# Two transformer blocks on one core: several attentions run as one chain of duos that begins under the value projections

## The reference

```python
# first block
h = rms_norm(x, norm_mix)
aq, ak, av, bq, bk, bv, cq, ckv, cg, mg = split(h @ w_in)
oa = diff_attention(norm(aq), norm(ak), av, lam, bias_a)       # 4 heads, two maps each, causal; then rms_norm
ob = banded_attention(norm(bq), norm(bk), bv, bias_b, 128, sinks)   # 8 heads, window 128
oc = nsa_attention(norm(cq), kc, vc, ks, vs, kw, vw, gates, bias_c) # 8 heads: compressed + selected + window
x = x + sum_n(sigmoid(mg_n) * (o_n @ w_branch_n)) @ w_out
x = x + relu(rms_norm(x) @ w_up)**2 @ w_down
# second block, twice
x = x + 0.5 * mod * swiglu(modulate(rms_norm(x)))
h = modulate(rms_norm(x))
qa, ka, va, ub, qc, kc, vc, f, g = split(h @ w_in)
ya = chunked_relpos_attention(norm(qa), norm(ka), va)          # 8 heads
yb = multiscale_pool(ub)
yc = forgetting_attention(norm(qc), norm(kc), vc, f)           # 8 heads
x = x + mod * (sum_n(sigmoid(g_n) * (y_n @ w_branch_n)) @ w_out)
x = x + 0.5 * mod * swiglu(modulate(rms_norm(x)))
```

## Time and profile before

| | |
|---|---|
| median of 3 runs | 3509.34 us (3509.17 to 3512.36) |
| the profiled execution | 3509.4 us |
| its span, first to last instruction | 3507.6 us |
| mean granted clock of PE | 0.992 |
| PE, POOL, DVE, ACT busy | 97%, 68%, 34%, 25% of the span |
| first block's values alone | about 76 to 98 us |
| attention A, B, C | about 98 to 232, 232 to 320, 320 to 552 us |
| A2 and C2 of the first layer | about 1459 to 1612, 1612 to 1782 us |

### The profile page before, as it was taken

One profiled execution on the slowest core, in us unless ns is written; L12 is line 12 of the kernel. 1 busy time (PEld: TensorE's weight loads), 2 busy tenths in 40 slices (PEclk: granted clock), 3 DMA queues, 4 the chain that ended last, 5 costly groups with the idle time before them and its releaser, 6 DMA issues.

```text
span 3507.6 us, 42466 instructions
## 1 busy us (share of the span) xinstructions
PE 3407.7 (97%) x17034; PEld 2738.9 (78%) x17034; DVE 1186.1 (34%) x2514; ACT 883.3 (25%) x1876; POOL 2370.5 (68%) x1242
## 2 busy tenths in 40 slices
PE   8978999999999999999999999999999999999999
PEld 6655777988898888667779888888887677798887
DVE  6554342433443234552223111332245422241111
ACT  2656552211120002354312000210012543221000
POOL 7514547787778776645677877687775546678775
PEclk9999999999999999999999999999999999999999
DMA  3212223344535442212232222254432222223232
GB/s 142 68 60 82 73 64 102 143 175 168 187 132 198 175 165 94 73 58 82 85 103 102 96 97 95 80 218 167 170 129 73 67 75 79 82 97 103 98 100 73
DMA packets 104771, 388.08 MB, mean 111 GB/s; under 512 B 12016, under 2 KB 12400, under 8 KB 98432
## 3 DMA queue, kind: packets, MB, share of 16 engines
q1 hardware_dynamic: 88272, 292.76, 25.3%
q10 hardware_dynamic: 16304, 92.62, 6.9%
HBM read 383.20 MB, written 2.13 MB: 110 GB/s over the span
## 4 chain that ended last, share of the span: by engine, by line
PE 91%; DVE 4%; ACT 4%; issue 1%; ACTq 0%; DVEq 0%
PE psum L1202 28%; PE psum L1204 27%; PE psum L1203 27%; PE psum L1275 2%; PE psum L1317 2%; PE psum L1292 2%; PE psum L1261 1%; DVE rs_t L1663 1%; DVE s_sb L1704 1%; ACT s_sb L1445 0%; ACT s_sb L1463 0%; ACT L1445 0%; ACT L1415 0%; PE psum L1253 0%; ACT rs_t L1415 0%
## 5 line engine op out<-in xcount | busy, mean ns | idle before, releaser
L1170 POOL TENSOR_TENSOR w_hi<-raw,ones 128x1024 fp32r<-128x1024 f32 (+2 forms) x593 | 1041.3, 1756 | 981.0 <-PE psum L1204 973.1
L1173 POOL TENSOR_TENSOR w_lo<-raw,w_hi 128x1024 fp32r<-128x1024 f32 (+2 forms) x593 | 1316.4, 2220 | 46.5
L1202 PE MATMUL psum<-h_hi,w_hi 128*128 128x512 f32 (+2 forms) x2912 | 1141.9, 392 | 30.5 <-DVE r L1679 20.5
L1204 PE MATMUL psum<-h_hi,w_lo 128*128 128x512 f32 (+2 forms) x2912 | 1106.2, 380 | 0.0
L1203 PE MATMUL psum<-h_lo,w_hi 128*128 128x512 f32 (+2 forms) x2912 | 1105.6, 380 | 0.0
L1202 PEld LDWEIGHTS psum<-h_hi,w_hi 128*128 128x128 f32 (+1 forms) x2912 | 550.3, 189 | 167.4 <-issue 33.9
L1204 PEld LDWEIGHTS psum<-h_hi,w_lo 128*128 128x128 f32 (+1 forms) x2912 | 550.1, 189 | 106.7
L1203 PEld LDWEIGHTS psum<-h_lo,w_hi 128*128 128x128 f32 (+1 forms) x2912 | 551.0, 189 | 101.0 <-issue 7.2
L1202 PE MATMUL psum<-a_hi,w_hi 128*128 128x512 f32 (+1 forms) x1064 | 392.5, 369 | 0.0
L1203 PE MATMUL psum<-a_lo,w_hi 128*128 128x512 f32 (+1 forms) x1064 | 391.9, 368 | 0.0
L1204 PE MATMUL psum<-a_hi,w_lo 128*128 128x512 f32 (+1 forms) x1064 | 391.8, 368 | 0.0
(11 more groups left out here) (198 smaller groups left out, 3305.0 us busy)
## 6 DMA issues: line engine op xcount, KB each, us to landing
raw<-weights_dram SPq DMA_DIRECT2D x487, 512.0 KB, 3.4
ada_t<-ada_dram ACTq DMA_DIRECT2D x48, 1536.0 KB, 7.1
raw<-weights_dram SPq DMA_DIRECT2D x76, 256.0 KB, 2.7
raw<-weights_dram SPq DMA_DIRECT2D x32, 384.0 KB, 3.1
bias_t<-biases_dram ACTq DMA_DIRECT2D x36, 256.0 KB, 2.9
bias_t<-cum_dram ACTq DMA_DIRECT2D x16, 256.0 KB, 4.1
out_dram<-x SPq DMA_DIRECT2D x8, 256.0 KB, 2.0
raw<-weights_dram SPq DMA_DIRECT2D x4, 408.0 KB, 3.2
```

Of the source, the lines that this page charges most:

```text
L1170: nc.gpsimd.tensor_tensor(high, piece, ones[:, 0:1].to_broadcast([P, n]), ALU.mult)\
L1173: nc.gpsimd.tensor_tensor(w_lo[:, p % NR, 0:n], piece, high.bitcast(F32), ALU.subtract)\
L1202: mm(dst, lh, rh, start=first, stop=False)
L1204: return mm(dst, ll, rh, start=False, stop=last)
```

## The change

The attentions of a block share one chain: `chain_of` lists the duos of A, B and C (or A2 and C2), and `attend(chain, kind)` gives the beats whose products belong to one kind, so that the scores of the next attention's first two duos stand in the last two beats of the one before. Only the last attention of a chain ends with `flush`. The beats -2 and -1 of the chain are put by `led` between and after the four value groups: in the first block score 1 after block 0, exp and probabilities 1 after block 1, score 2 after block 2, and exp 2, turn 1, copy 1 and probabilities 2 after block 3; in a layer score and exp of its first duo follow block 0. The values of a layer go to banks 6, 7, 5. B's woven groups lose bank 3. C takes `SUM_BANK` when its inverses are computed, and holds it until then. Scores whose root, or whose compressed keys, are not yet in the order take steps off `LATER` first. The rest of the diff is names.

```diff
--- before.py
+++ after.py
@@ -48,7 +48,7 @@
 
 SCORE_BANKS, T_BANKS, SUM_BANK, O_BANK = (0, 1), (2, 3), 4, 5
 BARE_RING = (5, 6, 7)
-MIX_RINGS = dict(att_a=(3, 6, 7), att_b=(3, 6, 7), att_c=(6, 7), att_a2=(6, 7), att_c2=(6, 7))
+MIX_RINGS = dict(att_a=(3, 6, 7), att_b=(6, 7), att_c=(6, 7), att_a2=(6, 7), att_c2=(6, 7))
 UP_FIRST = (6, 7, 4)
 MIX_FIRST, MIX_RING = (6, 7, 5), (0, 1, 3)
 UP_RING, DOWN_RING, C_BANKS = (2, 3, 0, 1), (4, 5), (6, 7)
@@ -173,6 +173,15 @@
         passed()
 
 
+def led(chain, groups):
+
+    parts = [part for part, _ in attend(chain, chain.duos[0].kind, True)]
+    out = []
+    for i, g in enumerate(groups):
+        out += [g] + parts[i * len(parts) // len(groups):(i + 1) * len(parts) // len(groups)]
+    return out
+
+
 def stretches(jobs):
 
     for job in jobs:
@@ -190,9 +199,10 @@
         pass
 
 
-def weave(kind, layer, jobs):
-
-    beats = attend(kind, layer)
+def weave(chain, kind, jobs):
+
+
+    beats = attend(chain, kind)
     total, weight = sum(job.n for job in jobs if isinstance(job, Group)), sum(w for _, w in beats)
     q, done, passed_by = stretches(jobs), 0, 0
     for beat, w in beats:
@@ -202,7 +212,8 @@
             done += next(q, total)
     for _ in q:
         pass
-    flush()
+    if chain.duos[-1].kind == kind:
+        flush()
 
 
 
@@ -504,16 +515,31 @@
     return (Q_AT[u.kind], 4 + u.pair)
 
 
-def attend(kind, layer):
-
-
-    duos = duos_of(kind, layer)
+@dataclass(eq=False)
+class Chain:
+
+    duos: list
+    masks: list
+
+
+def chain_of(kinds, layer):
+    return Chain([u for kind in kinds for u in duos_of(kind, layer)], [])
+
+
+def attend(chain, kind, lead=False):
+
+
+    duos, masks = chain.duos, chain.masks
     n = len(duos)
-    masks = []
+    own = [j for j in range(n) if duos[j].kind == kind]
+    lo, hi = own[0], own[-1] + 1
+    if lead:
+        lo, hi = -2, 0
 
     def scores(j):
         if j + 2 < n:
             u = duos[j + 2]
+            kind = u.kind
             u.n = tick("scores")
             for name in ("probs", "transposed", "pt_copied", "pv"):
                 assert tick(name) == u.n
@@ -522,8 +548,8 @@
             u.s_before = [take(b) for b in SCORE_BANKS]
             HELD[SCORE_BANKS[0]] = HELD[SCORE_BANKS[1]] = ("probs", u.n) if kind == "att_a" else ("row_min", 2 * u.n)
             u.need = max(READY[(Q_AT[kind], u.pair)], READY[keys_of(u)])
-            if kind == "att_c":
-                u.inv_before = take(SUM_BANK)
+            while u.need > ROOTED[0] or u.br == "cmp" and "kc_done" not in TOTAL:
+                LATER.pop(0)[1]()
             put("score", u)
             if u.last:
                 load_bias(u.bias.n + 2, 2 * u.n)
@@ -532,7 +558,7 @@
     def turns(j):
         if 0 <= j + 1 < n:
             u = duos[j + 1]
-            u.t_before = [take(b) for b in (T_BANKS[:1] if kind in ("att_a", "att_b") else T_BANKS)]
+            u.t_before = [take(b) for b in (T_BANKS[:1] if u.kind in ("att_a", "att_b") else T_BANKS)]
             for b in T_BANKS[:len(u.t_before)]:
                 HELD[b] = ("pt_copied", u.n)
             put("turn", u)
@@ -569,15 +596,19 @@
             put("exp", duos[j + 2])
 
     def low(j):
-        if 0 <= j and duos[j].last and kind != "att_a":
+        if 0 <= j and duos[j].last and duos[j].kind != "att_a":
             put("blow", duos[j])
 
     def scale(j):
         if j + 2 < n:
-            put("prob", duos[j + 2])
+            u = duos[j + 2]
+            if u.kind == "att_c":
+                u.inv_before = take(SUM_BANK)
+                HELD[SUM_BANK] = ("inverses", 2 * u.n)
+            put("prob", u)
 
     out = []
-    for j in range(-2, n):
+    for j in range(lo, hi):
         w = 1 + max([d.blocks for d in duos[max(0, j):j + 3]])
         if kind == "att_a":
             out += [(lambda j=j: scores(j), w), (lambda j=j: (exps(j), turns(j)), w),
@@ -588,7 +619,7 @@
         else:
             out += [(lambda j=j: scores(j), w), (lambda j=j: (exps(j), turns(j)), w),
                     (lambda j=j: (products(j), copy(j)), w), (lambda j=j: (low(j), scale(j)), w)]
-    return out + [(lambda: [mask_bias(b) for _, b in masks], 0)]
+    return out + [(lambda: [mask_bias(b) for _, b in masks], 0)] * (hi == n)
 
 
 
@@ -839,7 +870,8 @@
     k = [normed((l, "ka", i), "key", (l, 1), ("r0", 4 + i), MIX_RING) for i in range(4)]
     order = [q[0], k[0], q[1], k[1], q[2], k[2], q[3], k[3]]
     norm_rest(mix, in_banks(order[:3], MIX_FIRST))
-    run_all(order[3:] + token_groups((l, "va"), S, "v0", MIX_RING))
+    chain = chain_of(("att_a2", "att_c2"), l)
+    run_all(order[3:] + led(chain, token_groups((l, "va"), S, "v0", MIX_FIRST)))
     flush()
 
     ring = MIX_RINGS["att_a2"]
@@ -851,22 +883,22 @@
     steps = [pool_steps(g, ring) for g in range(4)]
     groups = [q[0], u[0], k[0], u[1], q[1], u[2], k[1], u[3], q[2], k[2], *token_groups((l, "vc"), S, "v1", ring),
               q[3], k[3]]
-    jobs, chain = [f], []
+    jobs, pooled = [f], []
     for g in groups:
-        jobs += [g] + chain[:2]
-        chain = chain[2:]
+        jobs += [g] + pooled[:2]
+        pooled = pooled[2:]
         if g is u[0]:
             jobs.append(forget)
         if g is k[0]:
             jobs.append(lambda: put("fstore"))
         if g in u:
             shifts, product = steps[u.index(g)]
-            chain += shifts + [product]
-    jobs += chain
+            pooled += shifts + [product]
+    jobs += pooled
     put("tables")
-    weave("att_a2", l, jobs)
+    weave(chain, "att_a2", jobs)
     ring = MIX_RINGS["att_c2"]
-    weave("att_c2", l, merge((l + 1, 1), "br_b", "set", ring) + merge((l + 1, 0), "br_a", "mid", ring))
+    weave(chain, "att_c2", merge((l + 1, 1), "br_b", "set", ring) + merge((l + 1, 0), "br_a", "mid", ring))
     if l == 0:
         tick("cond_loaded", 16)
         put("condload")
@@ -909,7 +941,8 @@
     put("signs")
     mask_bias(0)
     mask_bias(1)
-    run_all(order[2:] + [lambda: put("lam")] + token_groups(("av",), S, "v0"))
+    chain = chain_of(("att_a", "att_b", "att_c"), 0)
+    run_all(order[2:] + [lambda: put("lam")] + led(chain, token_groups(("av",), S, "v0")))
     flush()
 
     ring = MIX_RINGS["att_a"]
@@ -919,15 +952,15 @@
           normed(("ck", 4), "key", ("small", "gain", 7), ("k5", 2), ring),
           plain(("ck", 0), ("k5", 3), ring), plain(("ck", 1), ("k5", 4), ring)]
     tick("gate_tanh")
-    weave("att_a", 0, [ks[0]] + b + ks[1:] + token_groups(("vbc",), V_BC, "v_bc", ring)
+    weave(chain, "att_a", [ks[0]] + b + ks[1:] + token_groups(("vbc",), V_BC, "v_bc", ring)
           + [lambda: put("gates", TOTAL["plain_out"])])
 
     ring = MIX_RINGS["att_b"]
     cq = [normed(("cq", i), "query", ("small", "gain", 4), ("r2", i), ring) for i in range(4)]
     gather, hidden = compress(ring)
-    weave("att_b", 0, [lambda: gather(0), cq[0], lambda: gather(1), cq[1], hidden, cq[2], cq[3]])
+    weave(chain, "att_b", [lambda: gather(0), cq[0], lambda: gather(1), cq[1], hidden, cq[2], cq[3]])
     ring = MIX_RINGS["att_c"]
-    weave("att_c", 0, merge((0, 0), "br_a", "set", ring) + merge((0, 1), "br_b", "mid", ring))
+    weave(chain, "att_c", merge((0, 0), "br_a", "set", ring) + merge((0, 1), "br_b", "mid", ring))
     tick("cond_loaded", 16)
     put("condload")
     run_all(merge((0, 2), "br_c", "last"))
```

## The result

The changed kernel takes **3535.96 us** (median of 4 runs, 3534.75 to 3536.68) beside 3510.61 us for the kernel before in the same session: ratio 1.0077, 95% interval 1.0065 to 1.0089. It is 25 us slower, where 12 us faster was forecast; the range (3486 to 3512) does not hold it.

What follows compares the result with a forecast made beforehand. The prediction took TensorE (PE) as the bound, busy 3407.7 of 3507.6 us, so only its idle time could be removed. Its terms summed to -11.9 us, from 3509.4 to 3497.5 us, with a range of 3486 to 3512.

Steps and rivals of the forecast that it cites:

- Part 1: Duos 1 and 2 under the first block's values: new wait +3.9, old idle -0.4, moved work -3, duo 17 +0.5 us.
- I take -3: In A: 6.8 us of chunks moved into beats with 20.0 us idle save 3 us, between 0 and -6.8.
- Rival (b): Moved work is not absorbed, each beat grows by it; 3 + 1.5 + 3 us come back, 3505 us; chance 0.12.
- Part 2: Seam A to B: idle time and half-clock time won back, -8 us, between -2 and -10.9.
- rival (a): Seams give half, the old wait returning a beat later: -6.75 in place of -13.5, 3504.3 us; chance 0.15.
- Part 3: Inside B: moved chunks absorbed, -1.5 us; bank 3 leaving B's ring, +0.5 us.
- Part 4: Seam B to C: wait before score 34 and half clock won back, -5.5 us; last query's root late, +1 us.
- Part 5: Two layers: early score waits +2.3, moved chunks absorbed -1.5, seam A2 to C2 -0.5; +0.3 us each, +0.6 in all.
- rival (c): The clock stays up: three half-clock stretches inside A also go, 7.7 us more gained, 3489.8 us; chance 0.13.
- Neither sign of a wrong forecast: Forecast wrong if B's 16 beats grow by more than 4.1 us, or A2 by more than the 8.1 us moved in.
- (d): Slower: the layers' group starts meet banks held by roots sooner, 8.1 us per layer, 3517.7 us; chance 0.11.

Runs made afterwards that it cites:

- e3: The change with the fourth query group of C in bank 6 instead of bank 7; 3523.53 us, ratio 1.0038.
- e2: The change with the lead kept, each attention after the first on its own chain again, and bank 3 back in B's ring; 3548.33 us, ratio 1.0110.
- e7: The kernel before with one added PE wait per layer, after value block 0, for the last key's root; 3518.29 us, ratio 1.0022.
- e9: e8 with the first woven group of A and of A2 run whole before the first beat; 3509.31 us, ratio 0.9998.
- e6: The change with only the first block's attentions joined, no lead, C's fourth query group in bank 6, layers as in the kernel before; 3500.71 us, ratio 0.9975.
- e14: e6 with the pool's product of input 2 moved behind the first value group; 3485.32 us, ratio 0.9934.
- e5: The change without the lead, all attentions joined, with C's fourth query group in bank 6; 3502.13 us, ratio 0.9978.
- e13: e6 with the pool's product in A2 one place of the woven list later; 3513.34 us, ratio 1.0011.
- e18: e5 with the pool's products placed as in e15; 3485.90 us, ratio 0.9936.
- e10: The kernel before with B's woven groups in banks 6 and 7 alone, nothing joined; 3519.07 us, ratio 1.0025.
- e16: The kernel before with only the pool's product of input 2 moved behind the first value group; 3495.55 us, ratio 0.9961.
- e17: The change, lead as made, with the bank of e3 and the pool's products placed as in e15; 3496.23 us, ratio 0.9965.
- e15: e8 with the pool's product of input 1 moved behind input 3, that of input 2 behind the first value group; 3482.50 us, ratio 0.9924.
- e8: The change with C's fourth query group in bank 6, layers' lead from value block 1, first block's lead behind value blocks 0 to 2; 3511.79 us, ratio 1.0007.

## Why the prediction was wrong

By lengths, the forecast and the result were made up so (us; the second row is the change beside the kernel before, the bank by e3):

| | values and A, with the lead | ring of B | A's last product to C's, without the ring | two layers | sum |
|---|---|---|---|---|---|
| forecast | +1.0 | +0.5 | -14.0 | +0.6 | -11.9 |
| measured | +11.0 | +5.4 | -9.4 | +18.3 | +25.3 |

The steps that failed are the prices of the lead, in A and in the layers. New waits were priced at their own length, with nothing for the clock behind them and nothing for the waits that the shifted order would make.

- **Part 1, the first block's lead** (+1.0 us in all). The wait came as worked out: 3.72 us for the predicted 3.9. The step "I take -3", the moved 6.8 us taken in by A's idle time, was wrong: with the lead alone (e2) values and A take 157.6 us (154.8 before, 152.6 in e7), +2.8 or more, where the terms said +0.5 with the -3 and +3.5 without. Rival (b) had this. None of the terms or rivals had the rest: on the joined chain values and A take 165.8 us, +11.0. PE is idle there for 23.7 us (before 19.9) and busy at half clock for 30.1 us (before 15.5); 3.8 us and half of 14.6 us make 11.1. The idle time is cut otherwise: before, A had two waits over 3 us (3.69 and 5.57), the change has five (3.72, 3.33, 3.22, 4.06, 4.30). Why this comes on the joined chain alone is not shown; with the softer lead, fewer chunks in A's beats take most of it away (e9).
- **Part 2, seam A to B** (-8). Right in mechanism: the waits of 5.88 us and 2.60 us are gone, the clock over the seam is 0.99. With the bank mended the joined first block gives some 9 us by the times of e6 and e14, 6 us by lengths, where parts 2 to 4 said 13.5: half to two thirds of the forecast, near the 6.75 us of rival (a). Its old wait did not come back a beat later; in its place a product waits 1.8 to 3.0 us for its copy ahead of the seam B to C (e5, e6, e13, e14, e18; 1.9 us before).
- **Part 3, the ring of B** (+0.5). This term failed by itself: I bounded it by twice a wait of 2.60 us and took next to nothing, since the steps "keep their distance in chunks". They do not: when a group takes a bank whose root is not in the order yet, the plan pulls the root's steps forward, back to back. It costs 6.9 us of wait: 5.4 us of the first block's length (e3), 9 us of the whole time alone (e10) and 12 to 14 us in the change (e3). That line of `mm` (the loop on `ROOTED`) stood in the code before.
- **Part 4, seam B to C** (-5.5, +1). The wait at the seam went, but the wait of 6.94 us came at its place: the stretch 311 to 334 us has 14.45 us busy where it had 17.11. With the bank mended, A's last product to C's takes 308.1 to 310.7 us without a lead (e5, e6, e13, e14, e18), where it took 317.7, 315.0 and 315.4 (before, e7, e16).
- **Part 5, the layers** (+0.6, measured +18.3). The wait for the last key's root was 2.31 us as predicted; its price was not, 3.9 us instead of 2.3 (e7, interval 2.1 to 5.4). With the places mended on both sides (e17 beside e16) the layers cost 0.9 and 1.2 us more, near the forecast's +0.3 with the clock's 1.7. So the other terms held, and what failed is what they left out: moving 12 chunks shifted every later job by a beat or two, and the product of input 1, right behind its DVE steps as before, waited 4.24 us, since those steps now fell beside POOL's splits (4.91 us in place of 1.34). And I named the 5.5 us of bank waits in the earlier trace rows as idle time that might take in chunks; the 5.0 us of them are a fixed collision in the order (e16: 13.7 us without any join or lead).
- **The clock.** Parts 2 and 4 and rival (c) had it change, and only as a gain. The step that failed is the pricing of every new wait at its own length, while the trace of before already showed the stretches at half clock where PE waits. Half of what PE does more at half clock is 15.4 us, over half of the loss. The same reckoning gives what e14 to e16 win: 5.0 us of wait per layer, and 6.5 to 8.3 us of length.
- **The signs.** Neither sign of a wrong forecast came: from A's last product to B's it is 87.4 us (before 88.7), and from the copy of the last values to A2's last product 155.0 us (before 152.1). The loss stood in A, and in the layers' values with A2, which together grew from 174.2 to 183.2 us; no sign looked there.
- **The rivals.** (d), group starts that meet banks held by roots, was nearest: it set 8.1 us per layer, and the layers lost 8.8 and 9.5. It had 0.11, because DVE was busy for only 60.26 of 139 us. A mean load says nothing about a chain of steps that is pulled together. But that it came so near is in part luck: the waits that made it up were of another kind than it said, one for the pool's DVE steps, and the clock.

## What to carry to other kernels

In a ring of two banks, look for each short job: what runs right behind it gets the bank of what ran right before it. Where that is a group with a long tail (a root, a norm), move the short job, and read a wait that returns in each layer at the same place as a fault of the order, not as spare time. Price a wait of PE of the size seen here (2.2 us and up) at its length and, in addition, at half of what PE does in the stretch at half clock that may follow it; here such a stretch went with eight of ten waits of 2.2 to 2.3 us at a layer's first score. After any change of the order, read the list of waits again before the sum: the shift itself makes new ones.

## What the runs showed of the hardware

- A short wait can cost more than itself. With a wait of 2.2 to 2.3 us of PE at a layer's first score came a stretch of 3.41 us at a granted clock of 0.50, nearly all of it busy, in both layers of the change, e2, e7 and e17, and none in both layers of e3; the whole cost 3.9 us (e7), and the layers without the stretch were 1.7 us shorter (e3). With A2's waits of 4.2 to 5.5 us came 6.83 or 3.41 us. After A2 lost its waits over 2 us (e14, e15, e16) no stretch at 0.50 is left in the layers.
- A DVE instruction with two operands in SBUF (128x512, float32) took 0.69 us with POOL idle and 2.71 us beside POOL's splits of 128x1024; one of 128x16 took 0.17 and 1.71 us. The Trainium skill ("SBUF — State Buffer", SBUF: two separate sides) states that these two engines share a pair of ports, held by one of them for a whole instruction; the rows of e8 agree: the DVE instruction, begun 0.44 us after POOL's of 2.60 us, ends at 1523.24 us, and POOL's at 1522.69; the shorter one ends at 1520.04 us, and the split that it ran beside at 1520.02.
